# Window-attention steps: the filler projection moved ahead of the values and of the transposes of the probabilities

## What is computed

```python
def swa_sink_layer(h, w_in, sinks, w_out, kb, vb):
    proj = h @ w_in
    q, g = jnp.split(proj, 2, axis=-1)
    q = apply_rope(q.reshape(B, S, SWA_HEADS, SWA_HEAD_DIM), cos, sin)
    s = jnp.einsum('bnqgrd,bnkgd->bngrqk', qc, kb).astype(jnp.float32) * (SWA_HEAD_DIM ** -0.5)
    m = jnp.maximum(jnp.max(s, axis=-1, keepdims=True), sink)
    p = jnp.exp(s - m)
    probs = p / (jnp.sum(p, axis=-1, keepdims=True) + jnp.exp(sink - m))
    o = jnp.einsum('bngrqk,bnkgd->bnqgrd', probs.astype(vb.dtype), vb)
    y = o * jax.nn.silu(g)
    return y @ w_out
```

## Time and profile before

| | |
|---|---|
| median of 3 runs | 2462.72 us (2461.18 to 2463.23) |
| the profiled execution | 2461.14 us, span of its instructions 2459.3 us |
| busy: PE, DVE, ACT, POOL | 98%, 54%, 27%, 9% of the span |
| chain that ended last | PE 93%, DVE 4%, issue 1% |
| granted clock of TensorE | 0.999 of full speed |
| window loop of block 1 | from 1121.1 us on (block 0: from 507.8 us) |

### The profile page before, as it was taken

How to read it: one execution, slowest core, us unless ns; L and a number is a source line. 1 busy time by engine, 2 the same in 40 slices (tenths; PEclk the granted TensorE clock), 3 DMA queues, 4 the chain that set the end, 5 groups by cost and what they waited for, 6 DMA issues and landing times.

```text
span 2459.3 us, 29097 instructions
## 1 busy us (share of the span) xinstructions
PE 2422.2 (98%) x11408; PEld 1998.9 (81%) x11408; DVE 1336.3 (54%) x1954; ACT 663.7 (27%) x1454; POOL 216.5 (9%) x202
## 2 busy tenths in 40 slices
PE   7999999999999999999999999999999999999998
PEld 6888888877888888888888888888888888888886
DVE  6554655577555565555645444554654445445384
ACT  2312312235121212223512122122452221313143
POOL 2111111221010000100000000000000000001000
PEclk9999999999999999999999999999999999999999
DMA  8667565655786648653565454644256546454433
GB/s 345 267 240 291 197 264 218 244 188 201 271 331 258 256 189 306 237 190 120 207 238 207 189 222 153 232 159 161 101 219 255 226 159 234 158 224 164 171 103 146
DMA packets 67192, 525.17 MB, mean 214 GB/s; under 512 B 6176, under 2 KB 6944, under 8 KB 38432
## 3 DMA queue, kind: packets, MB, share of 16 engines
q1 hardware_dynamic: 58224, 487.85, 52.5%
q10 hardware_dynamic: 8880, 36.18, 4.0%
HBM read 404.47 MB, written 119.54 MB: 213 GB/s over the span
## 4 chain that ended last, share of the span: by engine, by line
PE 93%; DVE 4%; issue 1%; DMA 0%; ACT 0%; POOL 0%; DVEq 0%; SPq 0%; POOLq 0%
PE ps L561 30%; PE ps L563 30%; PE ps L562 29%; PE ps L885 2%; PE ps L708 1%; DVE ff L1636 1%; PE ps L895 1%; DVE fr L1249 1%; PE ps L628 1%; DVE mx L1676 1%; DVE xlo L1249 0%; DMA raw<-in_stream 0%; DVE ff L1706 0%; PE ps L825 0%; DVE whl L1296 0%
## 5 line engine op out<-in xcount | busy, mean ns | idle before, releaser
L561 PE MATMUL ps<-whl,xhi 128*128 128x512 f32 (+1 forms) x1408 | 543.2, 386 | 2.6 <-DVE xlo L1249 2.6
L563 PE MATMUL ps<-whl,xlo 128*128 128x512 f32 (+1 forms) x1408 | 536.8, 381 | 0.0
L562 PE MATMUL ps<-whl,xhi 128*128 128x512 f32 (+1 forms) x1408 | 535.1, 380 | 0.0
L561 PE MATMUL ps<-xhi,whl 128*128 128x512 f32 x768 | 304.3, 396 | 18.1 <-DVE xlo L1253 16.3
L561 PEld LDWEIGHTS ps<-whl,xhi 128*128 128x128 f32 x1408 | 265.1, 188 | 52.8 <-DVE xlo L1249 1.9
L563 PEld LDWEIGHTS ps<-whl,xlo 128*128 128x128 f32 x1408 | 264.7, 188 | 51.4
L562 PEld LDWEIGHTS ps<-whl,xhi 128*128 128x128 f32 x1408 | 265.2, 188 | 48.0
L563 PE MATMUL ps<-xhi,whl 128*128 128x512 f32 x768 | 300.7, 392 | 0.0
L562 PE MATMUL ps<-xlo,whl 128*128 128x512 f32 x768 | 300.0, 391 | 0.0
L561 PE MATMUL ps<-whl,fr 128*128 128x512 f32 x576 | 230.8, 401 | 2.1 <-DVE whl L1291 2.1
L563 PE MATMUL ps<-whl,fr 128*128 128x512 f32 x576 | 228.0, 396 | 0.0
(11 more groups left out here) (153 smaller groups left out, 3246.3 us busy)
## 6 DMA issues: line engine op xcount, KB each, us to landing
whl<-split_w SPq DMA_DIRECT2D x108, 2048.0 KB, 7.8
split_w<-whl SPq DMA_DIRECT2D x44, 2048.0 KB, 7.2
raw<-in_stream SPq DMA_DIRECT2D x52, 1024.0 KB, 9.4
whl<-split_w SPq DMA_DIRECT2D x30, 1024.0 KB, 8.0
whl<-comb_w SPq DMA_DIRECT2D x24, 1024.0 KB, 5.4
comb_w<-ff SPq DMA_DIRECT2D x16, 1024.0 KB, 6.3
fr<-comb_w SPq DMA_DIRECT2D x12, 1024.0 KB, 5.0
sx<-comb_w SPq DMA_DIRECT2D x12, 1024.0 KB, 9.0
```

Of the source, the lines that this page charges most:

```text
L561: pe.matmul(dst, lhs[0], rhs[0], start=start, stop=False)
L562: pe.matmul(dst, lhs[0], rhs[1], start=False, stop=False)
L563: return pe.matmul(dst, lhs[1], rhs[0], start=False, stop=stop)
```

## The change

In each step of the window loop `filler(s)` is called ahead of `values(s - 3)` and `transpose_p(s - 2)` and no longer behind them. Nothing else differs; the programs of the other engines are the same.

```diff
@@ -945,11 +945,11 @@
                         scores(s)
                     if 4 <= s < 8:
                         transpose_q(1, s - 4)
+                    filler(s)
                     if s >= 3:
                         values(s - 3)
                     if s >= 2:
                         transpose_p(s - 2)
-                    filler(s)
```

## The result

The changed kernel takes 2546.91 us (median; 2545.73 to 2547.36), against 2462.82 for the kernel before: a ratio of 1.0341 (95% interval 1.0321 to 1.0361). A fourth execution of the changed kernel took 4117.14 us at a mean granted clock of 0.559; the median counts it, the range and the ratio go by the other three. The prediction had the direction and missed the size: 2524 us, with 2540 as the upper end of its range. The profiled execution took 2546.47 us, 85.3 more than the profiled one of before.

What follows compares the result with a forecast made beforehand. TensorE (PE) was taken as the bound, the sum as waits alone: 44.4 us in blocks 1 to 3 plus 17.9 in block 0, 62.3 on the profiled 2461.1, median 1.6 above; about 2525, given as 2524, range 2510 to 2540.

Steps and rivals of the forecast that it cites:

- handover chain: Steps 4 to 7, every block: transposes to Q through ACT's copy, DVE's split and rotation, 4.00 us; PE waits 2.97.
- Q: PE's transposes of the queries; in steps 4 to 7 they wait for DVE's rotation, making such a step 7.91 us.
- Step 8: Every block: scores wait for ACT's store of queries behind copy and exponentials, 3.35 us from transposes instead of 0.36.
- Step 14: Filler (first output projection) waits for DVE's split of the gated tiles: +2.2 us in blocks 1 to 3, +2.3 in block 0.
- plain steps: Window-loop steps with no new wait of PE; predicted to stay at 4.76 us.
- The sum for a block: Blocks 1 to 3, each: 12.6 us from steps 4 to 8 plus 2.2 from step 14.
- Block 0: First block, where DVE also splits weight chunks: +17.9 us, with 15.9 and 20.2 as its ends.
- wait of the tail: Values after step 16 wait for the copy of step 17: +1.5 us in block 0, nothing in blocks 1 to 3.
- step 12's filler: Block 0: waits for step 11's chunk piece, 5.6 or 4.1 us by its length, middle 4.8; +3.4 net.
- Rival 1: TensorE's clock falls in the new waits: 26 waits at 2.4 us, +62, 2586 us; chance 0.05 in full.
- Rivals 2 to 4: Waits partly hidden, about 2499 us, chance 0.05; faster, 2450, 0.015; nothing changes, 2463, 0.015.
- rival 2: Part of the waits stays hidden: without step 8's term and a quarter of the others, about 2499 us; chance 0.05.

## Why the prediction was wrong in size and right in direction

**The handover chain: right.** From the transposes of the probabilities to Q it was to take 4.00 us, and it did (1169.38 to 1173.38). That was to give steps of 7.91; the measured fast one is 7.96 (1169.82 to 1177.78):

```profile
1169.38 0.60 PE L895 MATMUL ps<-idt,ff 128*128 128x128 f32 x4
1169.82 1.03 PE L885 MATMUL ps<-kwin,ff 128*128 128x256 f32 x4
...
1177.78 1.03 PE L885 MATMUL ps<-kwin,ff 128*128 128x256 f32 x4
```

The idle time reads 2.54 and not 2.97 because the trace lets the row of the scores run on 0.36 us beyond the point at which the next matmul could follow (1.03 long, 0.67 from start to start), and because the transposes took 0.44 and not 0.36. Step 8 was to take 3.35 from transposes to scores:

```profile
1204.37 0.60 PE L895 MATMUL ps<-idt,ff 128*128 128x128 f32 x4
...
1206.96 0.62 ACT L1163 ACTIVATE ff<-ps 128x512 f32<-128x512 f32 x1
...
1207.71 1.13 PE L885 MATMUL ps<-kwin,ff 128*128 128x256 f32 x4 [2.74 <-ACT ff L1163]
```

It took 3.34. In the kernel before the same chain took 3.35 too (1161.28 to 1164.63), but with the filler inside it. Step 14 of blocks 1 to 3 was there (1.79 us idle, 2.15 from start to start; 2.2 forecast), and plain steps stayed at 4.76. That doesn't follow from the forecast's own lengths, which add up to 4.58: the 0.18 us that the values gain behind the filler come back at the transposes (0.44) and the filler (2.94). The sum for a block was 14.8; without the clock it measured 14.6 to 14.9. The experiments on DVE's and ACT's order showed the cause and not only the size.

**Block 0: 17.9 forecast, 19.8 measured.** The wait of the tail was 1.32 (1.5 forecast), and steps 4 to 8 grew by 11.1 without their slow fillers (10.7). The wait at step 12's filler read 4.66, or 5.0 from start to start (4.8 forecast), and that is luck. The 4.8 was the middle between a long and a short piece of the chunk; the piece was short, which by the forecast gives 4.1, and the rest came from another DVE operation, ahead of the exponentials, that took 1.37 us in place of 0.16:

```profile
588.85 1.90 POOL L494 TENSOR_SCALAR whl<-raw 128x2048 fp32r<-128x2048 f32 x1 [7.01 <-DMA raw<-in_stream]
...
589.39 1.37 DVE L1680 SCALAR_TENSOR_TENSOR nm<-mx,nsink 128x4 f32<-128x4 f32 x1
...
593.44 1.13 DVE L1296 SCALAR_TENSOR_TENSOR whl<-raw,gain,whl 128x128 fp32r<-128x128 f32 x4
```

The term of the waits that was too small is step 14: 4.4 forecast, 6.38 read (6.7 from start to start).

```profile
604.20 2.15 POOL L494 TENSOR_SCALAR whl<-raw 128x2048 fp32r<-128x2048 f32 x1 [13.46 <-PE ps L563]
...
604.51 2.91 DVE L1291 TENSOR_TENSOR whl<-raw,whl 128x1024 fp32r<-128x1024 f32 x1
...
611.15 1.22 DVE L1291 TENSOR_TENSOR whl<-raw,whl 128x1024 fp32r<-128x1024 f32 x1
612.42 0.80 PE L561 MATMUL ps<-whl,fr 128*128 128x512 f32 x1 [6.38 <-DVE whl L1291]
```

The piece of step 12 took 2.91 us and not 1.22, and so everything on DVE up to the piece of step 13 (611.15) came later, by 1.7 us. Some 0.8 more would have been missing even so (an estimate from the same timeline): the row maximum of step 13 stands behind that piece and ahead of the split. The prediction had counted only the piece that is waited for, at its short length.

**The clock: wrong, and this is the step that failed.** The sum "consists of waits alone": it put the lower clock behind the new waits at nothing, and the range left 7 us for it. Rival 1 was described rightly, down to its sign ("matmuls spaced 0.43 us behind a wait"), and given 0.05 in full and "2 to 7 us" in part. It measured 21.1 us, which carries the time from 2526 (2461.1 + 64.2 + the distance to the median) to 2547. In full it was too dear as well, 62 us: not every wait brought the low level (14 of 26) and a fall cost 1.5 us and not 2.4, since the level mostly came back after seven or eight matmuls and not after the twelve of the earlier trace rows.

The argument against it was faulty in itself. It took the duration of the *first* matmul behind a wait (0.50 at 589.43 against 0.77 at 16.31) for the sign of the level. In the changed kernel the first matmul reads 0.48 at 1173.79 and also at 1181.76; one filler is fast and the other slow, and the fall shows from the third matmul on. In seven of the fourteen slow fillers it is so: the first spacing is the usual 0.31, and the fall comes later; in the other seven it is already 0.40 to 0.59. What would have told is the spacing of all twelve. At 589.43 that was indeed fast, but it was one wait, and of 2.10 us. The "about 4 us" of work between the waits are 4.9 by the forecast's own lengths. From a single wait shorter than all that were to come, no more followed than that the question was open; rival 1 in part deserved most of the chance, and the range should have reached from 2524 to some 2560, with the forecast inside it.

The Trainium skill, "TensorE: Matmul & The Clock Gate", section "HAM oscillation — how this bites in real kernels", says of a kernel whose waits for a DMA were longer than most of these that each burst of matmuls behind such a wait starts at the lower clock. This trace agrees in direction and not in measure: 14 of 26 bursts were slow, seven of these not from their first matmul, and waits of 2.54 us were followed by a slow filler in nine of fifteen cases.

**Rivals 2 to 4** didn't happen: no wait stayed hidden, nothing was won, and PE's order did set the time. (In rival 2 a quarter of the other terms is 12 to 13 us, not 14, which moves its time by under 2 us.)

## What to carry to other kernels

When work is moved on the engine that bounds, ask of each handover that it passes what the *other* engines, in their own order, have put between it and the work that comes back; here the length of that chain, read from four rows, gave the loss of blocks 1 to 3 to within 0.2 us each, apart from the clock. If the move takes away the cover of a chain, either the producer's program is reordered with it (two lines moved on DVE gave back 46 of 84 us) or the cover stays. And price new waits of TensorE twice, once for their length and once for the clock behind them, judged by the spacing of a whole run of matmuls and never by the first; work done for nothing in the wait can be cheaper than the wait.

## What the runs showed of the hardware

**What idle time stood ahead of the lower level.** Over the twelve traces, by the longest idle stretch between a filler of the window loops and the filler before it; a filler is called slow here if its first and last matmul start more than 3.3 us apart (usual: 2.5 to 2.8): 0.3 to 1.5 us, none of 59; 1.5 to 2 us, 4 of 43 followed by a slow filler; 2.0 to 2.6 us, 31 of 60; 2.6 to 3.0 us, 27 of 52; above 3.7 us, 31 of 31. Three more, behind 2.54 to 2.82 us, were slow in part and aren't counted. Equal waits of 2.54 us went both ways, often in turn from step to step. Why the one did and the other didn't stays open; no run was made to tell it. In the changed kernel a slow filler cost 1.0 to 1.6 us, mostly at seven or eight matmuls 0.43 apart; over all runs it was 0.7 to 2.2. The mean granted clock of the changed kernel agrees: a fall from 0.999 to 0.989 of full speed is 1% of 2545 us, 25 us, beside the 21 counted.

**DVE held up by GpSimd.** The prediction had said that no row told why one piece took 2.78 us and another 1.22. Rows of the kernel before, which it hadn't read, do:

```profile
574.04 2.23 POOL L494 TENSOR_SCALAR whl<-raw 128x2048 fp32r<-128x2048 f32 x1 [6.24 <-PE ps L563]
...
585.23 2.06 POOL L494 TENSOR_SCALAR whl<-raw 128x2048 fp32r<-128x2048 f32 x1 [8.97 <-PE ps L563]
```

```profile
585.44 1.86 DVE L1688 TENSOR_TENSOR den<-esum,esk 128x4 f32<-128x4 f32 x1
```

A DVE operation on 4 elements a partition took 1.86 us, against 0.15 a step earlier: it ended at 587.30, with GpSimd's (585.23 + 2.06 = 587.29). The piece at 574.41 ended at 577.19, 0.9 behind GpSimd's end of 576.27; the one at 604.51 at 607.42, 1.07 behind 606.35. The operation at 589.39 above ended at 590.76, with GpSimd's (590.75). In all four DVE's operation started behind GpSimd's and got through only when that was done. The Trainium skill, "SBUF — State Buffer", section "Who interferes with whom", says that a DVE instruction with two inputs in SBUF contends with a GpSimd instruction that reads SBUF, at a port that they share. These rows agree, and so does one of the kernel before with an input from PSUM (`fr<-ps,fr`, L1249): at 606.08, within a GpSimd operation of 605.67 to 607.58, it took its usual 0.69. No run here moved the one off the other, so this is read and not tried. GpSimd started these two roundings when PE released a chunk's buffer (`<-PE ps L563`), so the change moved what they collide with: the one at 585.23 fell between two pieces of a chunk, the one at 604.20 on a piece.
